# Merging the complex-rotate products of an S5 scan into 1024-wide VectorE instructions

## The reference

```
def _s5(u, s0, lam_re, lam_im, log_dt, b_re, b_im, c_re, c_im, d_skip, glu_w, glu_b):
    lam = lax.complex(lam_re, lam_im)
    dt = jnp.exp(log_dt)[:, None]
    lam_bar = jnp.exp(lam * dt)
    b_bar = ((lam_bar - 1.0) / lam)[:, :, None] * lax.complex(b_re, b_im)
    bu = jnp.einsum('gpc,btgc->btgp', b_bar, ug)
    ...
    _, s = lax.associative_scan(_scan_combine, (a, bu), axis=1)   # s[t] = lam_bar*s[t-1] + bu[t]
    y = jnp.real(jnp.einsum('gcp,btgp->btgc', c_mat, s)) + d_skip * uf
    g = jax.nn.gelu(y)
    out = g * jax.nn.sigmoid(g @ glu_w + glu_b)
    return out, s[:, t - 1]
```

## Time and profile before

| | us |
|---|---|
| median of two timed runs | 2882.89 |
| these runs | 2806.3 and 2959.48 |
| the profiled execution, slowest core | 2790.7 |
| its span, first to last instruction | 2789.2 |
| DVE busy in it | 1449.2 (52%) |
| PE busy in it | 1844.2 (66%) |
| POOL busy in it | 437.0 (16%) |

### The profile page before, as it was taken

One profiled execution on the slowest core, in us unless ns is written; L12 is line 12 of the kernel. 1 busy time (PEld: TensorE's weight loads), 2 busy tenths in 40 slices (PEclk: granted clock), 3 DMA queues, 4 the chain that ended last, 5 costly groups with the idle time before them and its releaser, 6 DMA issues.

```text
span 2789.2 us, 33490 instructions; the slowest of 8 cores (2756.8 to 2789.2 us)
## 1 busy us (share of the span) xinstructions
PE 1844.2 (66%) x11090; PEld 937.5 (34%) x11090; DVE 1449.2 (52%) x2340; ACT 1014.9 (36%) x1721; POOL 437.0 (16%) x501
## 2 busy tenths in 40 slices
PE   4423336899887589885633336688676864688685
PEld 2223324344333234432233334344333421343333
DVE  2689993656241466522579991555314315455322
ACT  1101113654332765522111114644324126654324
POOL 0022230012400011131023320000132000001130
PEclk7755567999998899897765657799897977798897
DMA  5130012367987045799010023233699650234794
GB/s 127 23 133 1 1 25 67 40 82 74 119 123 158 0 53 69 108 97 185 11 61 1 1 33 88 31 46 46 54 119 103 119 128 0 36 46 61 47 114 89
DMA packets 341426, 189.52 MB, mean 68 GB/s; under 512 B 199771, under 2 KB 321787, under 8 KB 340329
## 3 DMA queue, kind: packets, MB, share of 16 engines
q0 software_dynamic: 307360, 117.46, 38.5%
q1 hardware_dynamic: 33897, 69.91, 8.9%
HBM read 285.01 MB, written 22.03 MB: 110 GB/s over the span
## 4 chain that ended last, share of the span: by engine, by line
PE 29%; DVE 25%; issue 16%; DMA 15%; ACT 11%; POOL 2%; SPq 1%; DVEq 1%; ACTq 0%; POOLq 0%
PE bank L429 26%; DVE arena L435 15%; DVE arena L438 7%; DMA arena<-ffn_w_down 7%; ACT arena L452 6%; ACT arena L456 5%; PE bank L432 2%; DMA gsd<-arena 2%; DMA arena<-xp 2%; POOL arena L435 1%; ACT L452 1%; DMA arena<-sguwT 1%; SPq L116 1%; DMA arena<-ffn_w_gate 1%; DVE arena L444 1%
## 5 line engine op out<-in xcount | busy, mean ns | idle before, releaser
L429 PE MATMUL bank<-arena 128*128 128x512 bf16 (+2 forms) x9420 | 1651.7, 335 | 707.0 <-DVE arena L435 346.2
L429 PEld LDWEIGHTS bank<-arena 128*128 128x128 bf16 x9420 | 806.3, 106 | 1552.1 <-issue 934.5
L452 ACT ACTIVATE arena<-arena 128x512 f32<-128x512 f32 (+6 forms) x551 | 380.9, 695 | 506.9 <-DVE arena L438 356.6
L435 DVE TENSOR_TENSOR arena<-arena 128x512 bf16<-128x512 f32 (+7 forms) x754 | 403.9, 570 | 193.1 <-ACT arena L452 66.9
L435 DVE TENSOR_TENSOR arena<-bank,arena 128x512 f32<-128x512 f32 (+3 forms) x365 | 216.3, 647 | 313.9 <-PE bank L429 221.3
L438 DVE SCALAR_TENSOR_TENSOR arena<-arena 128x512 f32<-128x512 f32 (+1 forms) x448 | 286.9, 640 | 127.4 <-ACT arena L452 65.7
L435 DVE TENSOR_TENSOR arena<-arena,bank 128x512 bf16<-128x512 f32 (+4 forms) x422 | 244.7, 580 | 186.8 <-ACT arena L452 137.2
L456 ACT CAST arena<-arena 128x2048 bf16<-128x2048 f32 (+3 forms) x115 | 145.9, 1274 | 393.4 <-PE bank L429 171.8
L438 DVE SCALAR_TENSOR_TENSOR arena<-arena,bank 128x512 f32<-128x512 f32 (+1 forms) x160 | 87.2, 580 | 385.3 <-PE bank L429 385.2
L452 ACT ACT_TABLE_LOAD x61 | 78.3, 1283 | 511.0 <-PE bank L429 440.3
L452 ACT ACTIVATE arena<-bank,arena 128x512 f32<-128x512 f32 (+2 forms) x320 | 200.6, 627 | 94.7 <-PE bank L958 89.7
(11 more groups left out here) (29 smaller groups left out, 199.2 us busy)
## 6 DMA issues: line engine op xcount, KB each, us to landing
arena<-ffn_w_down POOLq DMA_DIRECT2D x128, 256.0 KB, 10.3
arena<-ffn_w_gate POOLq DMA_DIRECT2D x44, 512.0 KB, 7.5
arena<-ffn_w_up POOLq DMA_DIRECT2D x44, 512.0 KB, 9.6
arena<-xp SPq DMA_DIRECT2D x32, 512.0 KB, 4.5
arena<-gsd SPq DMA_DIRECT2D x48, 263.0 KB, 4.7
arena<-ffn_w_down POOLq DMA_DIRECT2D x64, 192.0 KB, 11.7
arena<-w_in_c POOLq DMA_DIRECT2D x16, 512.0 KB, 12.5
yp<-arena SPq DMA_DIRECT2D x16, 512.0 KB, 2.7
```

The source lines that it names most:

```text
L429: kb.op("pe", lambda e: e.matmul(out, lhsT, rhs, start=start, stop=stop), reads, writes)
L435: kb.op(eng, lambda e: e.tensor_tensor(out, a, b, op), reads, writes)
L452: kb.op("act", lambda e: e.activation(out, in_, func, **kw), reads, writes)
```

## The change

Pairs of DVE products that share a source become one instruction of twice the width. In `stage_M` the two products of `are` (by cos and by sin) are one product of 128 x 2 x 512: `are` is read twice by a step of zero, and the two tables, which lie one behind the other in the arena, are read through one view `CSV`. The same is done for `aim`. The scratch tiles become four of 128 x 2 x 512, used two at a time by turns; both POOL operations of a job now read one half of each. In `stage_D` the two halves of `WZ` are multiplied by cos in one instruction and by sin in another, so the four output products stand in another order, and the weights of two matmuls are exchanged to suit. `glu_back` is one instruction for all four blocks.

```
-        TM = [AR.f32([128, 512]) for _ in range(8)]
-        TM = [(a_, nbuf(r_)) for a_, r_ in TM]
+        TM2 = [AR.f32([128, 2, 512]) for _ in range(4)]
+        TM2 = [(a_, nbuf(r_)) for a_, r_ in TM2]
+        assert r_SIN0 - r_COS0 == 16 * LCH
+        CSV = AR_t[:, r_COS0:r_COS0 + 2 * 16 * LCH].rearrange("p (t a b) -> p t a b", t=2, a=16)
...
         def glu_back(c0, n, ti, gset):
             (GA32, b_GA32), (GAB, b_GAB), (SGG, b_SGG) = gset
-            for m in range(4):
-                TT("dve", YM[:, m, c0:c0 + n], GA32[:, m, :n], SGG[:, m, :n], ALU.mult, [b_GA32, b_SGG], [ymb[m][ti]])
+            TT("dve", YM[:, 0:4, c0:c0 + n], GA32[:, :, :n], SGG[:, :, :n], ALU.mult, [b_GA32, b_SGG],
+               [ymb[m][ti] for m in range(4)])
...
-                TT("dve", t1, are, cs, ALU.mult, [areb, b_COS], [t1b])
-                TT("dve", t2, aim, sn, ALU.mult, [aimb, b_SIN], [t2b])
-                TT("dve", t3, aim, cs, ALU.mult, [aimb, b_COS], [t3b])
-                TT("dve", t4, are, sn, ALU.mult, [areb, b_SIN], [t4b])
+                TT("dve", ta, are.unsqueeze(1).to_broadcast([128, 2, 512]), csn, ALU.mult, [areb, b_COS, b_SIN], [tab])
+                TT("dve", tb, aim.unsqueeze(1).to_broadcast([128, 2, 512]), csn, ALU.mult, [aimb, b_COS, b_SIN], [tbb])
                 emit_bu(job + 2)
-                TT(ADD_ENG, wre, t1, t2, ALU.add, [t1b, t2b], [b_W[0]])
-                TT(ADD_ENG, wim, t3, t4, ALU.subtract, [t3b, t4b], [b_W[1]])
+                TT(ADD_ENG, wre, ta[:, 0, :], tb[:, 1, :], ALU.add, [tab, tbb], [b_W[0]])
+                TT(ADD_ENG, wim, tb[:, 0, :], ta[:, 1, :], ALU.subtract, [tab, tbb], [b_W[1]])
...
-                srcs = ((zre, cs, 0, b_COS), (zim, sn, 1, b_SIN), (zre, sn, 0, b_SIN), (zim, cs, 1, b_COS))
-                for kk, (zz, tb, wi, tbb) in enumerate(srcs):
-                    eng_ = "pool" if (grp, kk) in DEMOD_POOL else "dve"
-                    TT(eng_, pp[:, kk, :], zz, tb, ALU.mult, [b_W[wi], tbb], [pk[kk]])
+                TT("dve", pp[:, 0:2, :], zz, cs.unsqueeze(1).to_broadcast([128, 2, 512]), ALU.mult,
+                   [b_W[0], b_W[1], b_COS], [pk[0], pk[1]])
+                TT("dve", pp[:, 2:4, :], zz, sn.unsqueeze(1).to_broadcast([128, 2, 512]), ALU.mult,
+                   [b_W[0], b_W[1], b_SIN], [pk[2], pk[3]])
...
                     MM(yo, CR[:, p, :], pp[:, 0, sl], False, False, [b_CR, pk[0]], [ybb])
-                    MM(yo, NCR[:, p, :], pp[:, 1, sl], False, False, [b_NCR, pk[1]], [ybb])
+                    MM(yo, NCI[:, p, :], pp[:, 1, sl], False, False, [b_NCI, pk[1]], [ybb])
                     MM(yo, NCI[:, p, :], pp[:, 2, sl], False, False, [b_NCI, pk[2]], [ybb])
-                    MM(yo, NCI[:, p, :], pp[:, 3, sl], False, j == 3, [b_NCI, pk[3]], [ybb])
+                    MM(yo, NCR[:, p, :], pp[:, 3, sl], False, j == 3, [b_NCR, pk[3]], [ybb])
```

More of the change, by code:

```diff
@@ L987, in mixer_even @@
         COS, r_ = AR.f32([128, 16, LCH]); b_COS = nbuf(r_)
+        r_SIN0 = AR.mark()
         SIN, r_ = AR.f32([128, 16, LCH]); b_SIN = nbuf(r_)
@@ L1287, in stage_M @@
                 aim, aimb = banks[(job % 2) * 2 + 1][:, :], bank_buf[(job % 2) * 2 + 1]
-                cs = COS[:, grp * 4:(grp + 1) * 4, :].rearrange("p a b -> p (a b)")
-                sn = SIN[:, grp * 4:(grp + 1) * 4, :].rearrange("p a b -> p (a b)")
-                (t1, t1b), (t2, t2b), (t3, t3b), (t4, t4b) = TM[(job % 2) * 4:(job % 2) * 4 + 4]
+                csn = CSV[:, :, grp * 4:(grp + 1) * 4, :].rearrange("p t a b -> p t (a b)")
+                (ta, tab), (tb, tbb) = TM2[(job % 2) * 2:(job % 2) * 2 + 2]
                 wre = WZ[:, 0, grp * 4:(grp + 1) * 4, :].rearrange("p a b -> p (a b)")
                 wim = WZ[:, 1, grp * 4:(grp + 1) * 4, :].rearrange("p a b -> p (a b)")
-                TT("dve", t1, are, cs, ALU.mult, [areb, b_COS], [t1b])
-                TT("dve", t2, aim, sn, ALU.mult, [aimb, b_SIN], [t2b])
-                TT("dve", t3, aim, cs, ALU.mult, [aimb, b_COS], [t3b])
-                TT("dve", t4, are, sn, ALU.mult, [areb, b_SIN], [t4b])
+                TT("dve", ta, are.unsqueeze(1).to_broadcast([128, 2, 512]), csn, ALU.mult, [areb, b_COS, b_SIN], [tab])
+                TT("dve", tb, aim.unsqueeze(1).to_broadcast([128, 2, 512]), csn, ALU.mult, [aimb, b_COS, b_SIN], [tbb])
                 emit_bu(job + 2)
-                TT(ADD_ENG, wre, t1, t2, ALU.add, [t1b, t2b], [b_W[0]])
-                TT(ADD_ENG, wim, t3, t4, ALU.subtract, [t3b, t4b], [b_W[1]])
+                TT(ADD_ENG, wre, ta[:, 0, :], tb[:, 1, :], ALU.add, [tab, tbb], [b_W[0]])
+                TT(ADD_ENG, wim, tb[:, 0, :], ta[:, 1, :], ALU.subtract, [tab, tbb], [b_W[1]])
             if not first:
@@ L1334, in stage_D @@
                 sn = SIN[:, grp * 4:(grp + 1) * 4, :].rearrange("p a b -> p (a b)")
-                zre = WZ[:, 0, grp * 4:(grp + 1) * 4, :].rearrange("p a b -> p (a b)")
-                zim = WZ[:, 1, grp * 4:(grp + 1) * 4, :].rearrange("p a b -> p (a b)")
+                zz = WZ[:, :, grp * 4:(grp + 1) * 4, :].rearrange("p c a b -> p c (a b)")
                 pk = PPK[grp]
-                srcs = ((zre, cs, 0, b_COS), (zim, sn, 1, b_SIN), (zre, sn, 0, b_SIN), (zim, cs, 1, b_COS))
-                for kk, (zz, tb, wi, tbb) in enumerate(srcs):
-                    eng_ = "pool" if (grp, kk) in DEMOD_POOL else "dve"
-                    TT(eng_, pp[:, kk, :], zz, tb, ALU.mult, [b_W[wi], tbb], [pk[kk]])
+                TT("dve", pp[:, 0:2, :], zz, cs.unsqueeze(1).to_broadcast([128, 2, 512]), ALU.mult,
+                   [b_W[0], b_W[1], b_COS], [pk[0], pk[1]])
+                TT("dve", pp[:, 2:4, :], zz, sn.unsqueeze(1).to_broadcast([128, 2, 512]), ALU.mult,
+                   [b_W[0], b_W[1], b_SIN], [pk[2], pk[3]])
                 ct = grp
```

## The result

| | before | changed |
|---|---|---|
| median, us (runs) | 2796.97 (21) | 2813.75 (22) |
| profiled execution, us | 2790.7 | 2808.93 |
| its span | 2789.2 | 2807.4 |

The ratio of changed to before is **1.0055, 95% interval 1.0038 to 1.0073**: 15.4 us slower, between 10.6 and 20.4. (With 21 runs of the kernel before in place of two, its median is 2797, so the far run of 2959 was a disturbed one; ratios are taken without such runs.)

The account below looks back on a forecast made before the run. DVE carries the period, but waits for PE and POOL decide; POOL's add start sets the scans. Two halves at +5.2 us make +10.4 on a base of 2798.5: 2809 us, range 2784 to 2893, the forecast's own 2795 to 2822.

Parts of the forecast that it names:

- nothing else changes: Outside the two S5 stretches: the edited lines lie only in S5, so the +10.4 us counts no change elsewhere.
- the steady period: Six periods a half, stage_D 0 to 5 with stage_M 2 to 7: +1.08 + 0.08 - 0.48 = +0.68 us each.
- Price of an instruction: DVE products: two of 512 merged into one of 1024 save 0.06 us, not the 0.14 that durations suggest.
- Late first add: stage_M, jobs 2 and 3: POOL's first add starts 2.57 us after DVE's job 2, not 1.49: +1.08 us.
- Jobs 0 and 1 and glu_back are worth nothing: Inside a period, their 0.24 and 0.21 us saved only lengthen DVE's wait for PE, 1.3 to about 1.8 us.
- The 14th matmul: End of stage_D: PE has 14 matmuls instead of 13 after DVE's last product, +0.08 us.
- Holding the scratch pairs: First two stage_M calls of a half: DVE waits for buffers POOL's adds still read; with the adds' delay, +1.13 us a call.
- The sum over the S5 part: Each half: +4.1 steady periods, +2.3 first two stage_M, -1.0 last two stage_D, -0.2 glu_back: +5.2 us, +10.4 in all.
- Full saving: Rival: the add queue doesn't end last or its later start is absorbed; all merges pay, -19 us; chance 0.11.
- only stage_D paying: Rival: in stage_M the adds' late start is made up, so stage_D's saving remains, -7 us; chance 0.14.
- the price by durations: Rival: each merge saves 0.14 us, an instruction's exposed cost exceeding the cadences, and adds keep up: -39 us; chance 0.05.
- The slow repeated operand: Rival: the step of zero makes a wide product take 2.16 us instead of 1.22, +150 us or less; chance 0.04.

Follow-up runs that it names:

- the third profiles: The kernel before and the changed kernel, both unchanged, each profiled and timed a third time: ratios 0.9994 and 1.0056 to before.
- the last three kernels: Against before, GLU matmuls recorded later: with stage_D and glu_back merged, 0.9919; also last stage_M add on VectorE, 0.9924; both moves without any merge, 0.9941.

## Why the prediction was right or wrong

**The direction and the mechanism in the S5 part were right; the step that failed is the last one of the sum, that nothing else changes.** The text forecast +10.4 us, all of it from the two S5 stretches, and held everything outside to be equal without giving a reason. Measured are +7.4 us inside (from the first product of stage_M to the last glu_back, both halves, mean of cores, three profiles of each kernel: 548.7 to 556.1) and +15.4 (10.6 to 20.4) in the whole. Inside, the term that was mis-sized is the steady period: +0.68 us forecast, +0.46, +0.36 and +0.39 measured in three pairs of profiles.

So the number in the S5 part was too large and that in the whole too small, and since the two errors pull opposite ways, it is partly luck that 2809 lies so near to 2813.75. The base was a choice too: the mean of the profiled and the lower run, 2798.5, where 21 runs give 2797. Beside the median of 2882.89 that was shown, though, 2809 reads as 2.6% faster, while the text forecasts slower; the number and the word didn't stand on the same base. The chance of 0.94 for "the same" holds by 2%, but the difference is clear of noise. The upper end of the range, 2893, leaned on the run of 2959 and told nothing.

- *Price of an instruction.* 0.06 us for two merged: eight wide products of stage_D take 10.64 us with the six small ones, for 11.19, so 0.55 less where 0.48 was forecast, 0.07 a merge. glu_back 11.25 - 10.64 = 0.61, so 0.20 less for 0.21. In stage_M, with an input from a bank, four wide ones take 4.61 us for the 4.87 of eight narrow, again 0.07 a merge: a larger saving where an input comes from a bank doesn't show.
- *Late first add.* +1.08 forecast, 2.56 - 1.49 = 1.07 in the rows, 1.06 in the mean of the periods. Shown by the runs with the whole, half and no merge in stage_M: 7.76, 7.25 and 6.73 us from job 2 to the scans.
- *Jobs 0 and 1 and glu_back are worth nothing* beside PE's chain: the chain from stage_D's end stays 7.01 us, and the gap grows from 1.33 to 1.80 in the mean (+0.5 forecast).
- *The 14th matmul*, +0.08: seen in the rows of PE, where 14 take 1.62 us (262.32) and 13 took 1.48, but not in the length of the chain, which is 7.01 us before and after. What makes up for it wasn't found; the share of periods at PE's higher rate is the same in this pair, 55 and 53 of 96.
- *Holding the scratch pairs*, first two stage_M calls: +1.13 forecast. From the first product to the scans the rows give +1.28 for both (11.61 for 10.33; 12.94 for 11.66), and the mean of the cores +1.28 and +1.26 in the first half, +1.20 and +1.04 in the second. The waits for the pairs, 0.55 and 0.15 us, are there; mis-sized by at most 0.15.
- *The sum over the S5 part.* +5.2 us a half forecast. Measured: first stage_M +1.3, first to last scan +3.5 (226.95 less 223.5, means of three profiles each), the two last stage_D calls and a glu_back 2 x -0.55 - 0.20 = -1.3: +3.5, so **+7.0 us in all**. Read to the start of the last glu_back, which waits for PE and ScalarE, the end of a half is only 1.0 us earlier, and the sum is the +7.4 above. In the period, the terms that are off are the products of stage_D (0.07 too little a period) and the 14th matmul (0.08 too much in the chain), and up to 0.06 us a period by which stage_M is reached earlier and whose place I didn't find: +0.46 a period in the first pair of profiles, +0.38 in the others, where +0.68 was forecast.
- *The rest of the 15.4.* Ratios of the three timings of the changed kernel, weighted by their intervals, come to 1.0059 with 0.0013 either way; of the two repeats of the kernel before, 1.0011 with 0.0021 either way. Taken against each other that is +13.5 us with 7 either way, where the S5 part explains 7; the 6 left, with 7 either way, can't be told from nothing. Without the repeats taken off it is 16.5 with 4 either way, and the 9 left are clear of nothing. The two kernels' outside parts, 2330 to 2362 and 2341 to 2366 us, overlap; the third profiles, both from one chip, differ by 3.8. The other runs bear on it: in all ten timings of an edited kernel the timed difference stands above the one that its S5 part shows, by 1 to 19 us, in the two repeats by 5 and -2. For the last three kernels, whose stage_M is narrow, the S5 part is 28, 37 and 27 us shorter and the timed whole, an estimate from the ratios, 23, 21 and 17. So a rest of this kind isn't a mark of the wide stage_M. What it is **stays open**; it is the step that the forecast put at nothing.
- *The rivals.* Full saving, only stage_D paying in this kernel, and the price by durations fall with the period of 33.9 us. The slow repeated operand falls with 1.215 us. Only stage_D pays when stage_M is left narrow (the run on stage_D alone), which is another kernel.

The measurement confirms the second of the two rules that the prediction weighed. The Trainium skill, Perfetto Trace Analysis (Optimizing Scalar/DVE Operations), says that where DVE isn't saturated but causes bubbles on other engines, smaller instructions may let work be completed sooner. The runs agree: in stage_M the narrow form is the faster by 1.1 to 1.3 us a call. Its other advice there, to group work if the engine is saturated, holds for stage_D, where DVE is: 0.7 us a period.

## What to carry to other kernels

Merging two instructions saves what the start-to-start cadence shows (0.07 us here), not what the durations suggest (0.14), and delays the first result by a whole instruction (1.07 us here). So merge where the engine itself sets the end and nobody waits for the first half, as in stage_D, and keep results small where they feed a queue that ends last, as POOL's adds. Before making an engine's work shorter, ask of each gap in its timeline who ends it: two moves of work, one of matmuls in PE's order and one of an add from POOL to DVE, took 13 us out of the S5 part of each half, and the merges that are good took 4. In the timed whole, an estimate from the ratios, 17 us arrived of the 27 that the two moves save in both halves, and 21 of 37 with the merges.

## What the runs showed of the hardware that was not expected

A DVE instruction with both inputs in the arena is held while a POOL add runs, before the change as after it. The carry's 128 x 16 sum that starts beside POOL's last add takes 1.16 us (275.64 to 276.80, POOL ends at 271.75 + 5.01 = 276.76) and the next one 0.19. Over all cores 120 such sums take 1.16 us in the changed kernel and 1.18 in the one before, and those alone 0.18. The first scan beside an add takes 5.39 instead of 4.41; an add of 512 takes 0.98 instead of 0.69. Products that read a bank are not held: over all cores 1.216 us beside POOL's adds and 1.215 without.

What this costs differs. In a steady period it is next to nothing, as the second carry sum waits for the fourth add by a semaphore of its own (the 0.41 us in the first rows above) and the scans stand behind it. In the first stage_M of the first half, which has no carry, the two scans take 9.71 us instead of 8.74.

```profile
274.25 2.50 POOL L435 TENSOR_TENSOR arena<-arena 128x512 f32<-128x512 f32 x2
...
184.70 5.39 DVE L1305 TENSOR_TENSOR_SCAN arena<-arena 128x2048 f32<-128x2048 f32 x1 [1.57 <-POOL arena L435]
```

The Trainium skill, SBUF — State Buffer (Who interferes with whom), describes the port pair that DVE and GpSimd share as an exclusive lock. By it the held instruction waits for the other's end, and the three rows agree.
